# Decoder layer on one core: attention merge in two steps and in pairs, two slots kept free behind V's transposes, w_o's loads spread, last chunk's norm and first norm placed anew

## The reference

```
h   = x + mixer(rms_norm(x, norm1_w))
out = rms_norm(h + conv_glu(rms_norm(h, norm2_w)), final_norm_w)

mixer: proj = xn @ w_in       (51 column tiles of 128, here "jobs")
  A) 3 groups of dilated window attention, 4 heads of 64 each; the three
     groups' outputs of a position are weighted by their softmax sums
  B) gated DeltaNet, 4 heads of 128, 8 chunks of 128 tokens in sequence,
     its output normalised per head (out_norm) and gated
  y = sigmoid(gate_a) * (o_a @ w_pa) + sigmoid(gate_b) * (o_b @ w_pb)
  return y @ w_o
```

## Time and profile before

| what | value |
|---|---|
| runs | 1721.68, 1728.36, 1726.41 us; median 1726.41 |
| the profiled execution's own time | 1723.12 us |
| its span, first to last instruction | 1721.4 us |
| PE busy | 1679.3 us (98%) |
| DVE, ACT, POOL busy | 40%, 29%, 31% |
| DMA | 136.62 MB, mean 79 GB/s |
| mean granted clock of PE | 0.996 |

### The profile page before, as it was taken

The page is one execution under the profiler, slowest core; times in us unless marked ns, Lnnn a source line. Parts: engine busy times, 40 slices in busy tenths (PEclk is TensorE's granted clock), DMA queues, the critical chain, the costliest instruction groups (busy, mean ns, idle before and its releaser), DMA issues.

```text
span 1721.4 us, 20663 instructions
## 1 busy us (share of the span) xinstructions
PE 1679.3 (98%) x8339; PEld 1400.6 (81%) x8339; DVE 681.9 (40%) x941; ACT 500.7 (29%) x644; POOL 540.7 (31%) x332
## 2 busy tenths in 40 slices
PE   6999999999999999998999999999999999999998
PEld 4888888888888888887778888888888888888886
DVE  5323223354454444644351432222223333444455
ACT  4422221223222333343122332222222222322333
POOL 4335231322222132232233432222222223344583
PEclk9999999999999999999999999999999999999999
DMA  4222431121221323433571121111111111321212
GB/s 162 80 81 74 141 85 48 48 62 45 56 54 50 90 82 98 124 109 92 183 263 57 78 70 49 49 49 49 49 49 49 49 49 49 128 61 50 61 56 98
DMA packets 173524, 136.62 MB, mean 79 GB/s; under 512 B 20388, under 2 KB 152972, under 8 KB 173452
## 3 DMA queue, kind: packets, MB, share of 16 engines
q1 hardware_dynamic: 173232, 135.53, 26.0%
q10 hardware_dynamic: 220, 0.09, 0.0%
HBM read 104.82 MB, written 30.77 MB: 79 GB/s over the span
## 4 chain that ended last, share of the span: by engine, by line
PE 93%; DVE 2%; ACT 1%; DMA 1%; issue 1%; POOL 0%; SPq 0%; DVEq 0%; ACTq 0%
PE acc L421 61%; PE acc L2049 7%; PE bank_ab L1263 6%; PE att_ps L2049 3%; PE bank_ab L2049 3%; PE acc L1631 3%; PE att_ps L1338 2%; PE bank_ab L1631 1%; PE att_ps L1631 1%; PE att_ps L1320 1%; PE att_ps L1331 1%; PE bank_ab L1261 1%; PE bank_ab L1288 1%; DMA w_raw<-in_w_pb_dram 1%; PE acc L429 1%
## 5 line engine op out<-in xcount | busy, mean ns | idle before, releaser
L421 PE MATMUL acc<-xh,w_high 128*128 128x512 f32 x1504 | 487.4, 403 | 0.0
L421 PE MATMUL acc<-xl,w_high 128*128 128x512 f32 x1504 | 469.6, 391 | 0.0
L421 PE MATMUL acc<-xh,w_low 128*128 128x512 f32 x1504 | 469.0, 391 | 0.0
L421 PEld LDWEIGHTS acc<-xl,w_high 128*128 128x128 f32 x1504 | 282.9, 188 | 60.4
L421 PEld LDWEIGHTS acc<-xh,w_low 128*128 128x128 f32 x1504 | 282.8, 188 | 60.5
L421 PEld LDWEIGHTS acc<-xh,w_high 128*128 128x128 f32 x1504 | 272.0, 189 | 55.5 <-issue 7.5
L1963 DVE SCALAR_TENSOR_TENSOR u_conv<-acc,prm,u_conv 128x1023 f32<-128x1023 f32 x88 | 112.8, 1282 | 325.2 <-ACT u_conv L1876 319.1
L832 POOL TENSOR_TENSOR w_low<-w_raw,w_high 128x1024 fp32r<-128x1024 f32 x49 | 117.0, 2388 | 345.8 <-ACT w_high L914 345.8
L1934 POOL TENSOR_TENSOR w_low<-w_raw,w_high 128x1024 fp32r<-128x1024 f32 x42 | 100.9, 2403 | 352.4 <-ACT w_high L1839 352.4
L1876 ACT ACTIVATE u_conv<-acc,prm 128x1024 f32<-128x1024 f32 x44 | 53.1, 1207 | 310.7 <-PE acc L421 310.7
L1942 POOL TENSOR_TENSOR f_gl<-glu,f_gh 128x1024 fp32r<-128x1024 f32 x40 | 98.0, 2452 | 106.0 <-ACT f_gh L1851 105.9
(11 more groups left out here) (303 smaller groups left out, 2250.7 us busy)
## 6 DMA issues: line engine op xcount, KB each, us to landing
w_raw<-in_w_in_dram SPq DMA_DIRECT2D x51, 512.0 KB, 4.6
w_raw<-in_w_up_dram SPq DMA_DIRECT2D x44, 512.0 KB, 3.9
w_raw<-in_w_down_dram SPq DMA_DIRECT2D x44, 256.0 KB, 2.6
conv_d<-so SPq DMA_DIRECT2D x16, 512.0 KB, 3.0
gate_d<-qk SPq DMA_DIRECT2D x16, 512.0 KB, 3.1
g_gates<-gate_d SPq DMA_DIRECT2D x8, 1024.0 KB, 5.5
qk<-in_x_dram SPq DMA_DIRECT2D x8, 512.0 KB, 8.4
ckqk<-conv_d SPq DMA_DIRECT2D x8, 512.0 KB, 5.2
```

Source lines behind the costliest of these rows:

```text
L421: mm = nc.tensor.matmul(out[:, lo:hi], w, xx[:, lo:hi], start=first and j == 0, stop=last and j == 2)
```

## The change

1. **Attention merge.** `cmb` is cut in two: `cmbA` (maximum and differences on DVE, the exponential on ACT) and `cmb` (the rest on DVE). Two tiles go together: at slot 0 of jobs 43, 45, 47 and 49 stand `cmbA` of both; `cmb` and `cmbT` of the first stand at k = 4 and 7 of that job, those of the second at k = 1 and 4 of the next. The small buffers `cbs` and `cbm` exist twice. SP loads tile i + 2 at `cmbT` of tile i.
2. **V.** After a `vT` at slot s no attention item stands before slot s + 2. All later attention items move; the last `a_pv` goes from job 41, k = 3 to job 42, k = 4.
3. **Last chunk.** The norm of chunk 7 is an item of its own, `nv`, at k = 3 of job 48; `ob` of chunk 7 moves from job 50, k = 1 to job 49, k = 3. `FIRST_DIRECT` is 7, so chunk 6 is stored and loaded again too.
4. **w_o.** Its four first transfers are issued one behind each of the loads for m = 2 to 5.
5. **First norm.** x's third tile is loaded ahead of the first weights; DVE scales tile i before it takes the mean square of tile i + 1; ACT squares tile i + 3 right behind the split of tile i, and splits the second weight tile at i = 2, not i = 1.

```
--- before.py
+++ after.py
@@ -93,17 +93,17 @@
         ob = [("ob", c - 1)] if c else []
         out += [("vq", c)] + kt + [("P4", c)] + kT + [("T4", c)] + kkD + rest + [("P5", c)] + ml + [("T5", c)] + ob + sv0
         out += [("P6", c)] + sv1 + [("kS", c)] + sv2 + ts + [("T6", c), ("vn", c)] + tl + [("so", c)] + ex
-    return out + rest * 7 + [("ob", NT - 1)]
-
-
-OFF_PE = ("load", "ml", "sv0", "sv1", "sv2", "ts", "tl", "ex")
+    return out + rest + [("nv", NT - 1)] + rest * 3 + [("ob", NT - 1)]
+
+
+OFF_PE = ("nv", "load", "ml", "sv0", "sv1", "sv2", "ts", "tl", "ex")
 def att_units():
     return [(g, i) for g in range(NG) for i in range(NT)]
-FIRST_DIRECT = NT - 2
+FIRST_DIRECT = NT - 1
 def mixer_schedule(jobs):
@@ -112,10 +112,10 @@
     items = [("w", 0)]
     ready = []
     units = att_units()
-    combine = [(name, i) for i in range(NT) for name in ("cmb", "cmbT")]
+    combine = {}
     free_slot = 0
-    GAP = {"a_qk": 3, "a_pT": 2, "a_pv": 1, "cmb": 4, "cmbT": 4}
+    GAP = {"a_qk": 3, "a_pT": 2, "a_pv": 1}
     for n, (kind, t, _) in enumerate(jobs):
         for k in range(KT):
             items.append(("mm", n, k))
@@ -129,6 +129,7 @@
                     items.append(("silu", n - 1))
                 if pk == "v":
                     items.append(("vT", pt))
+                    free_slot = max(free_slot, n * KT + k + 2)
                     if pt % 2:
                         g = pt // 2
                         for u in units:
@@ -152,10 +153,17 @@
             slot = n * KT + k
             if kind == "gate" and t == 0 and k == 0:
                 free_slot = max(free_slot, slot + 3)
-            if slot >= free_slot and (ready or kind == "gate" and combine):
-                items.append((ready or combine).pop(0))
-
-                free_slot = slot + GAP[items[-1][0]] + (4 if items[-1] == ("a_pv", units[-1]) else 0)
+            if slot >= free_slot and ready:
+                items.append(ready.pop(0))
+                free_slot = slot + GAP[items[-1][0]]
+                if items[-1] == ("a_pv", units[-1]):
+
+                    for i in range(NT):
+                        start = (n + 1 + i // 2 * 2) * KT
+                        combine.setdefault(start, []).append(("cmbA", i))
+                        combine[start + (9 if i % 2 else 4)] = [("cmb", i)]
+                        combine[start + (12 if i % 2 else 7)] = [("cmbT", i)]
+            items += combine.pop(slot, [])
             if n > 1 + 3 * NH and dn and k % 2 == 1:
                 if dn[0][0] == "rest":
                     dn.pop(0)
@@ -278,8 +286,8 @@
         load_x(0)
         sp.dma_start(n1w, norm1_w.to_broadcast([P, D])).then_inc(s_n1w, 16)
         load_x(1)
+        load_x(2)
         load_w(0)
-        load_x(2)
         load_x(3)
         load_w(1)
         for i in range(4, NT):
@@ -308,11 +316,11 @@
             if i == 0:
                 act.wait_ge(m_raw[0], 16)
                 nc.scalar.activation(wh[:, 0, :, 0:2 * NH], raw[:, 0, :, 0:2 * NH], ACT.Copy).then_inc(m_whi, 1)
-            if i == 1:
+            if i + 3 < NT:
+                square(i + 3)
+            if i == 2:
                 act.wait_ge(m_raw[1], 16)
                 nc.scalar.activation(wh[:, 1], raw[:, 1], ACT.Copy).then_inc(m_whi, 1)
-            if i + 3 < NT:
-                square(i + 3)
     def constants(pool):
         nc.gpsimd.memset(mhalf, -0.5).then_inc(s_id, 1)
@@ -350,10 +358,10 @@
         mean_square(0)
         dve.wait_ge(s_n1w, 16)
         for i in range(NT + 1):
+            if i < NT:
+                scaled(i)
             if i + 1 < NT:
                 mean_square(i + 1)
-            if i < NT:
-                scaled(i)
             if i:
                 low(i - 1)
             if i == 2:
@@ -457,7 +465,7 @@
     ob_no = count([it for it in items if it[0] == "osplit" or it in direct])
     last_pv = ("a_pv", att_units()[-1])
     first_split = [it for it in items if it in ob_no][0]
-    assert order[last_pv] < order[("cmbT", 0)] and order[("dn", "so", FIRST_DIRECT)] < order[first_split]
+    assert order[last_pv] < order[("cmbT", 0)] and order[("dn", "so", NT - 2)] < order[first_split]
     unit_no = count(att_units())
     stores = [u for u in att_units() for _ in range(2 if u[0] == 2 else 1)]
     o_stored = {u: 16 * (n + 1) for n, u in enumerate(stores)}
@@ -524,8 +532,8 @@
         O = sb(ctx, "O", [P, AH, OC])
         assert nc.sbuf_base >= rows_at[-1] + D * 4
         mx = sb(ctx, "mx", [P, 2, AH])
-        cbs = sb(ctx, "cbs", [P, 4, NG, AH])
-        cbm = sb(ctx, "cbm", [P, 4, AH])
+        cbs2 = [sb(ctx, f"cbs{j}", [P, 4, NG, AH]) for j in range(2)]
+        cbm2 = [sb(ctx, f"cbm{j}", [P, 4, AH]) for j in range(2)]
         rows_at.append(nc.sbuf_base)
         ckqk1 = sb(ctx, "ckqk1", [P, 2 * NH, P])
         rows_at.append(nc.sbuf_base)
@@ -732,12 +740,12 @@
                     m = jobs[it[1]][1]
                     sp.wait_ge(s_taken, it[1] + 1)
                     sp.dma_start(gate_d[m], gate[m % 2]).then_inc(s_gst[m % 2], 16)
-                if kind == "cmb":
+                if kind == "cmbT":
                     i = it[1]
-                    if 0 < i < NT - 1:
-
-                        sp.wait_ge(s_co, i)
-                        load_outputs(i + 1)
+                    if i + 2 < NT:
+
+                        sp.wait_ge(s_co, i + 1)
+                        load_outputs(i + 2)
                 if kind == "oload":
                     c = it[1]
                     sp.wait_ge(s_obst, 16 * (c + 1))
@@ -887,14 +895,14 @@
                         g.tensor_tensor(on[:], o1[:], o1[:], ALU.mult).then_inc(s_osq, 1)
                     if name == "T4" and c:
                         out_norm(c - 1)
-                    if name == "ob" and c == NT - 1:
+                    if name == "nv":
                         out_norm(c)
                 if it in ob_no:
                     c = it[-1]
                     source = stage_o[:, c % 2] if kind == "osplit" else ckz[:]
                     if it == first_split:
-                        pool.wait_ge(s_dn, dn_done[("so", FIRST_DIRECT)])
+                        pool.wait_ge(s_dn, dn_done[("so", NT - 2)])
                     pool.wait_ge(s_obh, ob_no[it])
                     g.tensor_tensor(b_part(ol, c), source, b_part(oh, c).bitcast(F32),
                                     ALU.subtract).then_inc(s_obl, 1)
@@ -1010,8 +1018,9 @@
                     act.wait_ge(s_atpe, att_no[it])
                     g.activation(PT[:, 0:nb, :].rearrange("p b c -> p (b c)"), att_ps[:, 0:nb * P],
                                  ACT.Copy).then_inc(s_attk, 1)
-                if kind == "cmb":
+                if kind == "cmbA":
                     i = it[1]
+                    cbs = cbs2[i % 2]
                     act.wait_ge(s_cd, i + 1)
                     g.activation(cbs[:, 1], cbs[:, 0], ACT.Exp, scale=ATT_SCALE).then_inc(s_ce, 1)
                 if kind == "cmbT":
@@ -1218,15 +1227,18 @@
                                   att0[:, 0:AH * (DH + 1)].rearrange("p (h c) -> p h c", h=AH)).then_inc(s_attk, 1)
                     g.tensor_copy(O[:, :, DH + 1].rearrange("p (i a) -> p a i", a=2),
                                   mx[:, 0, :].rearrange("p (a i) -> p a i", a=2)).then_inc(s_o, 1)
-                if kind == "cmb":
+                if kind == "cmbA":
                     i = it[1]
-                    X = cb[i % 2]
+                    X, cbs, cbm = cb[i % 2], cbs2[i % 2], cbm2[i % 2]
                     dve.wait_ge(s_cl[i % 2], 16 * (i // 2 + 1))
                     top = X[:, :, :, DH + 1]
                     link(g.tensor_tensor(cbm[:, 0], top[:, 0], top[:, 1], ALU.max))
                     link(g.tensor_tensor(cbm[:, 1], cbm[:, 0], top[:, 2], ALU.max))
                     g.tensor_tensor(cbs[:, 0], top, cbm[:, 1].unsqueeze(1).to_broadcast([P, NG, AH]),
                                     ALU.subtract).then_inc(s_cd, 1)
+                if kind == "cmb":
+                    i = it[1]
+                    X, cbs, cbm = cb[i % 2], cbs2[i % 2], cbm2[i % 2]
                     dve.wait_ge(s_ce, i + 1)
                     link(g.tensor_tensor(cbs[:, 2], cbs[:, 1], X[:, :, :, DH], ALU.mult))
                     link(g.tensor_tensor(cbm[:, 0], cbs[:, 2, 0], cbs[:, 2, 1], ALU.add))
@@ -1474,13 +1486,13 @@
         for m in range(2, KT):
             load(m)
-            if m == 3:
+            if m == 2:
                 for j in range(2):
                     sp.wait_ge(x_gst[j], 16 * KT)
                 sp.wait_ge(x_co, NT)
-                for j in range(KT // PAIR):
-                    load_w(0, j)
+            if m - 2 < KT // PAIR:
+                load_w(0, m - 2)
         for st in range(NT):
             sp.dma_start(h[st][:, :], xd[st * P:(st + 1) * P, :]).then_inc(s_x, 16)
```

72 lines of the change are left out of this document (42 added, 30 removed).

## The result

| | before | after |
|---|---|---|
| median of 6 runs, us | 1721.8 | 1710.1 |
| lowest to highest | 1719.5 to 1728.36 | 1709.38 to 1712.72 |
| profiled execution's own time | 1723.12 | 1711.0 |
| its span | 1721.4 | 1709.3 |

The ratio is 0.9923, 95% interval 0.9907 to 0.994: faster by 11.7 us in the medians, and by 12.1 between the two profiled executions. The forecast was 1705.6, with a gain of 20.8. The time lies in the range, 4.5 above the forecast; the gain is 9.1 smaller than forecast, only a bit over half of it. The difference between 4.5 and 9.1 is the base: the median of 1726.4 that I started from rested on three runs, and with three more it is 1721.8. So the time came out closer than the gain by luck: a base that was 4.6 too high hid half of the miss.

What follows compares the result with a forecast made beforehand. PE was taken as the bound, busy 1679.3 of 1721.4 us. Gains 4.7 + 11.2 + 3.9 + 1.7 + 1.9 = 23.4, less losses 1.2 + 1.4 = 2.6, gave 20.8: 1705.6 from a median of 1726.4, range 1699 to 1715.

Steps and rivals of the forecast that it cites:

- V's transposes: Attention: two free slots behind V's transposes remove three PE waits for the copy of V; gain 4.7 us.
- Merge and last norm: Jobs around the merge and chunk 7's norm: PE's waits of 5.3, 2.4 and 3.5 us go; gain 11.2.
- The clock: Two half-speed stretches of PE behind the longest inner waits go with those waits; gain 3.9 us, bounds 0 and 3.9.
- the forecast's own signs of being wrong: Over 3 us wait in job 43, PEclk of 0.5 behind 30 us, or over 5 us of waits at `a_pT`.
- w_o: Weight loads: spreading w_o's four transfers removes PE's wait for w_low, caused by w_pb queued behind them; gain 1.7 us.
- First norm: Start: earlier scaling and transposes, tile 4's at about 20.4 us, clock rise moving along; gain 1.9, bounds 0 and 3.2.
- Job 43: DVE there is full and the pair's loads come later: PE waits 2.4 us, not 1.2; loss 1.2, bounds -1.2 and +4.
- Attention re-spaced: Moved attention units: new waits at (0, 2) and (0, 5), 1.9 less an old 0.5; loss 1.4, bounds -0.5 and +5.
- rival A: Waits move: job 43 and attention lose 4 + 5 us and a low clock stretch returns; 1714.2 us, chance 0.2.
- B: Rival: the start and the clock give nothing; gain 15.0, 1711.4 us, chance 0.13.
- C: Rival: ACT reaches the pair's exponentials only after the next gate's evacuation, so `cmb` still waits; 1720.7 us, chance 0.07.
- D: Rival, slower: late pair loads make DVE block P4 or P6 in four pairs, 24 us; 1738.6 us, chance 0.02.

Runs made afterwards that it cites:

- e1: The changed kernel without the two free slots behind V's transposes; median 1706.51 us, ratio to the kernel before 0.9908.
- e3: The kernel before with the paired attention merge alone; median 1711.62 us, ratio to the kernel before 0.9938.
- e5: The kernel before with only the last chunk's norm placed by itself; median 1717.55 us, ratio to the kernel before 0.998.
- e10: The changed kernel itself measured once more, with no edit; median 1709.21 us, ratio to the kernel before 0.9909.
- e4: The kernel before with the change of the first norm alone; median 1719.88 us, ratio to the kernel before 0.9999.

## Why the forecast was right and wrong

- **V's transposes, gain 4.7:** right, those waits are gone. But taken with its consequences the part most likely loses: e1 is 2.7 to 3.6 shorter without it, of which waits of PE explain 1.1.
- **Merge and last norm, gain 11.2:** right, every wait of it gone, and e3 and e5 show it part by part: 10.2 for the merge (its waits of 7.3, the rest clock and chance), 3.4 to 3.9 for the norm.
- **The clock, gain 3.9:** the two old stretches went and two others came in the profiled execution, so 0.5 there. This is close to the lower bound of 0. The reasoning "with both long waits gone both stretches go" had the wrong form: e3 and e10 have no low stretch with waits of 3.5 and 2.8 us in them, the changed kernel's profile has one with no wait before it. It also met one of the forecast's own signs of being wrong, a PEclk of 0.5 behind 30 us. What removing long waits seems to do is to make low stretches rarer: the runs of before span 6 to 12 us in each group, those of the changed kernel 3.3 and 1.8.
- **w_o, gain 1.7:** right as a wait; too small to be timed by itself.
- **First norm, gain 1.9:** the transposes came where forecast (8.00, and 19.89 where 20.4 was said), the clock's rise did not come 2 us earlier. In this execution 1.6 of the 2.5 us were left behind the rise; the low stretch at 45.5, counted above, took as much again. e4's profile kept 2.4.
- **Job 43, loss 1.2:** the wait at T6 is 1.13 ("about 1" was said), and P6 and kS added nothing in this execution. The second load landed 3.2 us behind T5's operations, as forecast (3). Net nothing lost in this execution; the landing's spread, 0 to 2.6 us of waits over the profiles, was not foreseen.
- **Attention re-spaced, loss 1.4:** **this step failed.** It was 7.8. I had gone through all 24 units with each operation's usual duration. The two units that I named wait 1.33 and 1.60 where I said 0.9 and 0.8, and the old wait of 0.5 that was to go stayed. The 2.82 at unit (1, 3) I did not see at all, since I took each operation at its usual duration and none on DVE takes 2.4 us; it is a small solve that happens to meet POOL's split, as one did in the trace before. And the reuse of `att_ps` behind the copy to `O` (two of 0.60), with d_kd (0.64) and d_T_vn (0.2), I had taken for covered. The upper bound of 5 was too low too, so rival A with its "4 + 5" was right in kind for this half only. The profiled gain (12.1) missed the forecast's 20.8 by 8.7 us: this step makes 6.4 of that (7.8 against 1.4) and the clock 3.4 (0.5 against 3.9), while job 43, better than forecast by 1.3, takes some of it back.

Of the rivals, A described the profiled execution best in the attention and in the low stretch that a new wait brings back, and not in job 43; its 1714.2 is 4.1 above the result as the forecast is 4.5 below. B said that the start and the clock give nothing (they gave 2.1 of 5.8 in this execution) and gave 1711.4, the nearest number; that is luck, since it left the attention's loss out: by the base of 1721.8 it would have been 1706.8. C's delay did not occur, and D's late loads cost 0 to 2.6 us, not 24.

## What to carry to other kernels

A gap put into an order written by hand moves everything behind it against every other engine's work: price it by the waits that it makes, not only by the one it removes, and try it alone and left out. Where a small operation on DVE may lie beside a large one of POOL and both read SBUF, give it POOL's whole duration (2.4 us here for 0.2) in the plan, or place it elsewhere; moving sv0 by one slot or the split by three took 2.2 to 2.8 us of waiting away here, and the later place of sv0 brought 1.8 of it back. Look through the trace for operations that are far longer in one place than in all others: they were there before the change. A term of a few microseconds that rests on the granted clock belongs in the range, not in the sum.
